# A two-block network on one core: whole banks of deferred projections in the first layer's attention and gated scan

## The reference, cut to what matters

```python
def _mixer_ab(h, w_in, gate_up, gate_bias, norm_gain, w_out, rel_bias):
    proj = jnp.einsum('bsd,df->bsf', h, w_in)
    qa, ka, va, qb, kb, vb, lr_f, lr_b, gate = _split(proj, ...)
    oa = dilated_attention(heads(qa, 8), heads(ka, 8), heads(va, 8), rel_bias)
    g_f = log_sigmoid(lr_f @ up[0] + gb_[0]) / 16
    g_b = log_sigmoid(lr_b @ up[1] + gb_[1]) / 16
    ob = bidirectional_gated_scan(qh, kh, heads(g_f, 4), kh, heads(g_b, 4), heads(vb, 4))
    ob = _head_rmsnorm(ob, norm_gain)
    y = jnp.concatenate([oa, ob], axis=-1) * jax.nn.silu(gate)
    return jnp.einsum('bsf,fd->bsd', y, w_out)
```

## Time and profile before

| what | value |
|---|---|
| median of 3 runs | 4887.4 us (4880.81 to 4889.06) |
| the profiled execution, its own time | 4883.06 us |
| span of the profiled execution | 4881.4 us |
| mean granted clock of TensorE | 0.873 of full speed |
| TensorE matmul busy | 3791.2 us, 78% |
| VectorE, ScalarE, GpSimd busy | 1612.8, 1071.5, 1035.2 us |

### The profile page before, as it was taken

One profiled execution on the slowest core, in us unless ns is written; L12 is line 12 of the kernel. 1 busy time (PEld: TensorE's weight loads), 2 busy tenths in 40 slices (PEclk: granted clock), 3 DMA queues, 4 the chain that ended last, 5 costly groups with the idle time before them and its releaser, 6 DMA issues. The chain is left out here.

```text
span 4881.4 us, 48054 instructions
## 1 busy us (share of the span) xinstructions
PE 3791.2 (78%) x17093; PEld 2453.1 (50%) x17093; DVE 1612.8 (33%) x3690; ACT 1071.5 (22%) x2169; POOL 1035.2 (21%) x915
## 2 busy tenths in 40 slices
PE   7799988997989999999979299952254386635994
PEld 3546766753455666556844165731244384232441
DVE  1012224332513434454312200047467653042103
ACT  0023333322413332333233200002212120010111
POOL 0000003221413333333324400000243241110112
PEclk8899999998999999999989599965577687857997
DMA  3233222355411111111142322225312143424996
GB/s 96 86 101 89 78 76 69 104 166 212 152 45 41 57 46 45 45 44 51 46 179 116 106 76 66 86 73 156 104 63 68 49 156 126 165 86 168 316 319 208
DMA packets 418577, 528.93 MB, mean 108 GB/s; under 512 B 71827, under 2 KB 320187, under 8 KB 418356
## 3 DMA queue, kind: packets, MB, share of 16 engines
q1 hardware_dynamic: 379443, 477.63, 29.5%
q10 hardware_dynamic: 34304, 31.64, 1.9%
q0 software_dynamic: 4608, 16.78, 1.4%
HBM read 387.09 MB, written 138.87 MB: 108 GB/s over the span
## 5 line engine op out<-in xcount | busy, mean ns | idle before, releaser
L622 PE MATMUL hgrn_ps_w<-xT,hgrn_ring 128*128 128x512 f32 x1152 | 507.0, 596 | 0.0
L594 POOL TENSOR_TENSOR hgrn_queries<-hgrn_qd,hgrn_pair_decay 128x640 f32<-128x640 f32 x192 | 285.3, 1504 | 414.9 <-PE hgrn_ps_a L673 198.5
L622 PEld LDWEIGHTS hgrn_ps_w<-xT,hgrn_ring 128*128 128x128 f32 x1152 | 216.7, 192 | 251.3 <-issue 251.3
L1139 PE MATMUL end_ps_z<-end_w,end_yT 128*128 128x512 f32 x768 | 338.4, 601 | 4.2 <-ACT end_yT L1088 2.4
L618 PE MATMUL hgrn_ps_w<-hgrn_ring,xT 128*128 128x256 f32 x1536 | 337.8, 379 | 0.0
L618 PEld LDWEIGHTS hgrn_ps_w<-hgrn_ring,xT 128*128 128x128 f32 x1536 | 289.0, 190 | 38.2 <-issue 0.5
L1139 PEld LDWEIGHTS end_ps_z<-end_w,end_yT 128*128 128x128 f32 x768 | 146.5, 193 | 186.1 <-issue 180.2
L240 DVE COPY in_stage<-in_ps 128x512 f32<-128x512 f32 (+3 forms) x47 | 29.1, 619 | 589.9 <-PE in_ps L184 455.2
L774 DVE COPY_PREDICATED hgrn_scores<-hgrn_mask,hgrn_ps_s 128x128 f32<-128x128 uint32 x192 | 48.4, 296 | 467.9 <-issue 465.9
L346 PE MATMUL gla_bg_ps<-gla_bg_w,xT 128*128 128x256 f32 x768 | 173.9, 386 | 5.3 <-DMA gla_bg_w<-in_w_in_ab_dram 5.3
L346 PEld LDWEIGHTS gla_bg_ps<-gla_bg_w,xT 128*128 128x128 f32 x768 | 147.9, 194 | 33.4 <-DMA gla_bg_w<-in_w_in_ab_dram 6.9
(11 more groups left out here) (550 smaller groups left out, 6948.3 us busy)
## 6 DMA issues: line engine op xcount, KB each, us to landing
expw_wg<-in_exp_w_gate_dram SPq DMA_DIRECT2D x16, 2048.0 KB, 10.7
expw_wu<-in_exp_w_up_dram SPq DMA_DIRECT2D x16, 2048.0 KB, 16.6
expw_wd<-in_exp_w_down_dram SPq DMA_DIRECT2D x16, 2048.0 KB, 22.2
gla_bg_w<-in_ada_w_dram SPq DMA_DIRECT2D x24, 1024.0 KB, 5.3
hgrn_ring<-in_w_in_c_dram SPq DMA_DIRECT2D x36, 512.0 KB, 4.0
in_wbuf<-in_w_in_dram SPq DMA_DIRECT2D x15, 1024.0 KB, 6.5
end_gt<-gate_l SPq DMA_DIRECT2D x16, 768.0 KB, 7.2
hgrn_ring<-in_w_in_c_dram SPq DMA_DIRECT2D x12, 1024.0 KB, 5.4
```

The costliest lines, as they stand in the source:

```text
L594: pool.tensor_tensor(queries[:, d, s, :].rearrange("p (b a c) -> p b a c", b=POINTS, a=PC), q, f, ALU.mult).then_inc(queries_done, 1)
L622: last = pe.matmul(bank[:, :], wt[:, k, 0:P], xT[:, k, part * BANK:(part + 1) * BANK], start=(k == 0), stop=(k == KB - 1))
L1139: made = pe.matmul(ps_z[h][:, :], yT[:, k, :], w[:, k, h * BANK:(h + 1) * BANK], start=(k == 0), stop=(k == NB - 1))
```

## The change

In `Background.__init__` the step `g` is worked out once for each bank, at its first matmul, and no longer for each matmul. A bank now lies whole in the step in which it would have begun; the steps up to the next bank's beginning get none.

```diff
@@ -262,8 +262,8 @@
         self.ended_in = []
         spent = 0
         for f in range(len(self.fills)):
+            g = f if f < lead else lead + min(slots - 1, spent * slots // total)
             for i in range(self.count(f)):
-                g = f if f < lead else lead + min(slots - 1, spent * slots // total)
                 if self.work[g] and self.work[g][-1][0] == f:
                     self.work[g][-1][2] = i + 1
                 else:
```

## The result

The changed kernel takes 4991.72 us in the median of four runs (4986.98 to 4995.29) against 4884.89 us for the kernel before; the ratio is 1.0218, with a 95% interval of 1.0200 to 1.0236. It is slower by 107 us. The forecast was slower by 140 (5028 us, range 4938 to 5080): right in sign and mechanism, too high by a third. The profiled execution took 4986.98 us, 4.7 under its median. The kernel before has got a fourth run (4882.38 us), so its median is now 4884.89 and not the 4887.4 from which the forecast was counted; its profiled execution, 4883.06 us, stands 1.8 under it.

What follows compares the result with a forecast made beforehand. The prediction took TensorE as the bound, with projections filling the time in which VectorE and ScalarE answer. Profiled 4883.1 + 56.3 waits + 84 clock = 5023.4; as the profile stood 4.3 us under the median, about 5028 us, range 4938 to 5080.

Steps and rivals of the forecast that it cites:

- The plan: Attention: 28 banks whole in 28 of 96 steps, 68 steps empty; gated scan the same, bank for bank, at no cost.
- The waits: Attention: score waits for VectorE's `att_shift` behind 65 empty steps, 0.88 us each wide, 0.83 narrow; 56.3 us.
- The copy on ScalarE: Attention: `bg.move` delays the turn by 0.2 us, swallowed by score's wait; costed at nothing, otherwise up to 0.5 us per bank.
- The clock: Attention: TensorE's clock falls to 1.2 GHz once before nearly each of 28 banks, 3.0 us each; 84 us.
- rival 1: Attention: waits alone, stretches dense enough to keep the clock up; 4943.7 us, chance 0.20.
- Rival 2: Attention: the clock falls only in narrow stretches, two banks of each head pair, 8 x 3.0 = 24 us; 4967.7 us, chance 0.15.
- Rival 3: Attention: the clock stays down through whole banks, 229 us; 5172.7 us, chance 0.06.
- Rival 4: Attention: faster, 68 fewer bursts save up to 8.2 us and the copy's 0.6 at the end; 4878.6 us, chance 0.04.

Runs made afterwards that it cites:

- the clock held, the kernel with the filler: Changed kernel plus one unread 128x256 matmul in each of 65 empty steps that have a bank to come; 4945.45 us, ratio 1.0123.
- the one run, the run with the later copy alone: Changed kernel with only ScalarE's copy of a bank (`bg.move`) one step later; 4990.08 us, ratio 1.0221.
- in the other: Changed kernel with VectorE's move_out behind the next bias and ScalarE's bank copy one step later; 4885.33 us, ratio 1.0008.
- the run with the filler in patterns 2 and 3: Changed kernel plus one unread matmul only in empty steps whose score is strided or narrow; 4943.50 us, ratio 1.0126.

## Why the prediction was right or wrong

**The plan** was read rightly. 28 banks, 68 empty steps, the scan the same: its 457 us did not move.

**The waits** were right in place and number, and in price to 7%. Forecast: 65 waits of score for `att_shift`, 56.3 us. Found: 66 in the list, one of them the old one at the start, and 60.4 us in the stage with the clock held. The 4 us above the forecast were not traced to single steps. The steps are 3.05 us wide, 3.63 strided and 2.47 narrow, as worked out from distances in steps that had no such wait. The prediction could be this close because every piece of the loop (values to `att_shift`, the hop to score, score itself) stood as a row in the trace of before, hidden but at its full length.

**The copy on ScalarE**, costed at nothing behind the score's wait and at up to 0.5 us for each bank if that were gone: nothing in the one run, 0.3 us behind some of the banks in the other.

**The clock** is the step that failed, as a size. The text said that "the clock falls once before nearly each bank", 28 times, at 3.0 us each, 84 us; measured are 45.8. In the records of the changed kernel the clock falls 15 times after the start of the stage, and 45.5 / 15 = 3.0 us, the price of the forecast. That the price came out is in part luck, for its two parts did not: 2.2 us of each fall lie in the step of the bank (forecast 1.68), 0.8 in the empty steps (forecast 1.35). The falls are longer than the one at the start from which the price was read, 8.9 us in the mean against 3.4, but an empty step that is slow throughout loses 0.8 to 1.0 us and not 1.2 to 1.5. The number of falls is what was off. It never fell in pattern 1 (clock 1.00 in 431.80 to 462.70, and 0.94 in the first stretch only for the old fall at the start). It fell in pattern 3 in all four head pairs and in pattern 2 in the first and the third (0.78), but not in the second (1.00 in 462.70 to 500.10) nor in the fourth (1.00 in 718.80 to 756.30). Counted by banks: ahead of the banks of steps 3 and 6 no fall in four pairs each, ahead of those of steps 10 and 13 four falls of eight, ahead of those of steps 17 and 20 and of the next pair's first bank eleven of eleven. I put all empty steps into one class because their busy shares lie close together, 62 to 67%. They differ in what they stream: a pattern 1 step has the same matmuls as one of pattern 2 in 3.05 us instead of 3.63, and a pattern 3 step has half the columns in 2.47. That this is the reason was not tested.

Why the clock fell in pattern 2 of one head pair and not in the next is open, but it is not the plan. The first and second pair have the same kind of projections there (L342), the third and fourth the other (L346). And the run with the later copy alone, whose TensorE has the same work, fell 16 times and at other places. The stretch with the banks of steps 10 and 13 in the first pair, in the changed kernel and in this run, and then this run's second pair from the bank of step 6 to that of step 13:

```profile
334.02:377.89 43.87, 40.75 (x147) 25.23 (x145) 8.01 (x42) 11.60 (x37) 0.00 (x0) 0.73 0.16 48
334.00:370.90 36.90, 32.56 (x147) 19.09 (x145) 8.00 (x42) 11.81 (x37) 0.00 (x0) 1.00 0.18 58
449.30:506.70 57.40, 54.24 (x179) 31.86 (x177) 9.20 (x48) 14.41 (x44) 0.00 (x0) 0.73 0.11 31
```

This run's first pair kept its clock and its second did not, the reverse of the changed kernel, though both executions came to the stretch in the first pair at the same time (334.0 us) and had the same steps since the first values. One of the 16 falls, and the one in the run with the filler in patterns 2 and 3, came ahead of the bank of step 6, where the changed kernel's clock held in all four pairs. So the 15 falls are those of one execution; in both executions the eleven places of pattern 3 fell.

**The Trainium skill's two sentences** ("TensorE: Matmul & The Clock Gate"). Its table of goals, in the section "Why this matters for your kernels", puts falls down to idle gaps between bursts. Here no wait of TensorE in the list was longer than 1.7 us, and the clock fell 15 times. The trace does not agree that avoiding long gaps is enough, and rival 1, which followed from it (4943.7 us), is what the kernel with the filler took (4945.45) and not what the changed one took. That transposes do not count as busy time in the same way (the Trainium skill, the same page, "Part 4: PE-mode transpose") was not tested apart from the other matmuls.

**The rivals.** Rival 2 (only the narrow stretches, 4967.7) had the right idea that the patterns differ and took too few: half of the places in pattern 2 fell as well, and pattern 3 has eleven falls and not eight, since the last empty steps of a pair stand ahead of the next pair's first bank. Rival 3 did not come: the clock was back within each bank. Rival 4's saving by fewer bursts exists in the 48 wide steps only, 48 x 0.06 = 3 us and not 8. The result lies between rival 2 and the forecast.

**The sum** with the terms as measured: 4884.9 + 60.4 + 45.8 = 4991.1, against 4991.7. This is no test of the division, since the two terms were made to add up to the attention's 106.2 us; it says that nothing outside the attention is needed.

## What to carry to other kernels

Background work that fills the waits of a chain is worth its place in every step, not its amount: before lumping it, find in the trace how long the chain would take alone (here 3.05 us against 2.17) and multiply by the steps that lose their cover. If lumps can't be avoided, look for the operation that stands in the chain only by an engine's order; moving one copy behind one bias took back 92 of 107 us. And test a suspected clock loss by adding work into the waits: if the kernel gets faster, the clock was part of the loss.

## What the runs showed of the hardware

- Adding 65 matmuls of 128x256 to a stage made the kernel 46 us faster (4991.72 to 4945.45): a stage whose TensorE was 90% busy by its records (461.19 of 511.28 us), with no wait in the list longer than 1.7 us, ran at a mean clock of 0.86, and at 1.00 with the filler.
- At the lower clock values lasted 1.97 us instead of 1.10 and turn 1.06 instead of 0.60, while a score with queries and keys read at a stride of four kept 1.28 us: its length did not follow the clock.
- With each bank in two bursts of 3.4 us in neighbouring steps, and one or two empty steps behind them, the clock's loss hardly shrank (40.7 against 45.8 us, 17 falls against 15). Bursts between thin steps did not hold the clock; a filler matmul of 0.43 us in the empty steps did.
- Two executions with the same work on TensorE, which reached the same steps at the same time (334.0 us), differed in whether the clock fell there (mean 0.73 and 1.00).
